# Decoder block with a 32-expert MoE in float32: consecutive weight rows per partition, and another order of work in the expert loop

## What is computed

```
logits = tok @ w_router + b_router;  vals, idx = top_k(logits, 4);  gates = softmax(vals)
for each of 32 experts:
    hgu   = tok @ w_gate_up[e] + b_gate_up[e]        # 1024 -> 2048, gate and up interleaved
    x_glu = min(hgu[:, 0::2], 7);  x_lin = clip(hgu[:, 1::2], -7, 7)
    act   = x_glu * sigmoid(1.702 * x_glu) * (x_lin + 1)
    acc  += gate[:, e] * (act @ w_down[e] + b_down[e])  # 1024 -> 1024
out = rms_norm(h + acc, g_final)
```

## Time and profile before

| what | us |
|---|---|
| runs of the kernel | 1122.81, 1123.18, 1124.02; median 1123.18 |
| profiled execution, its span | 1120.4 |
| profiled execution, its own time | not shown apart; the runs lie 2.4 to 3.6 above the span, their median 2.8 |
| TensorE busy | 1034.1 (92%) |
| VectorE, ScalarE, GpSimd busy | 253.4, 124.5, 45.2 |
| bytes moved | 420.09 MB, mean 375 GB/s |

### The profile page before, as it was taken

The page is one execution under the profiler, slowest core; times in us unless marked ns, Lnnn a source line. Parts: engine busy times, 40 slices in busy tenths (PEclk is TensorE's granted clock), DMA queues, the critical chain, the costliest instruction groups (busy, mean ns, idle before and its releaser), DMA issues.

```text
span 1120.4 us, 13552 instructions
## 1 busy us (share of the span) xinstructions
PE 1034.1 (92%) x5259; PEld 483.3 (43%) x5259; DVE 253.4 (23%) x648; ACT 124.5 (11%) x236; POOL 45.2 (4%) x85
## 2 busy tenths in 40 slices
PE   4979989999999999999999999999999999999995
PEld 3868454443444444433334444444444444444432
DVE  4886532111111111111111111111111111111102
ACT  2304321000000000000000000000000000000002
POOL 4830000000000000000000000000000000000000
PEclk9989979999999999999999999999999999999998
DMA  9972269999999999999999999999999999999891
GB/s 246 327 317 80 116 266 405 407 400 418 419 418 417 418 418 418 417 417 417 418 417 418 419 418 418 419 363 417 417 419 419 418 419 418 418 418 418 354 397 39
DMA packets 91783, 420.09 MB, mean 375 GB/s; under 512 B 7194, under 2 KB 23610, under 8 KB 58994
## 3 DMA queue, kind: packets, MB, share of 16 engines
q1 hardware_dynamic: 90646, 418.52, 93.0%
q0 software_dynamic: 1040, 1.20, 0.4%
q10 hardware_dynamic: 76, 0.09, 0.0%
HBM read 418.73 MB, written 1.05 MB: 375 GB/s over the span
## 4 chain that ended last, share of the span: by engine, by line
PE 88%; DVE 5%; ACT 4%; issue 1%; DMA 1%; SPq 0%; DVEq 0%
PE bank L1023 39%; PE bank L1053 20%; PE bank L996 11%; PE bank L1063 6%; DVE reg L621 4%; PE bank L882 3%; PE bank L928 2%; ACT reg L516 2%; ACT reg L518 2%; PE bank L1017 2%; PE bank L1041 1%; PE bank L1034 1%; DMA gu_ring<-in_conv_ln_b 1%; PE bank L864 0%; PE bank L1087 0%
## 5 line engine op out<-in xcount | busy, mean ns | idle before, releaser
L1023 PE MATMUL bank<-gu_ring,reg 128*64 128x512 f32 x2048 | 447.3, 594 | 0.0
L1023 PEld LDWEIGHTS bank<-gu_ring,reg 128*64 128x64 f32 x2048 | 145.9, 138 | 282.8 <-issue 277.3
L1053 PE MATMUL bank<-dn_ring,reg 128*64 128x512 f32 x1024 | 226.8, 595 | 26.8 <-ACT reg L516 26.8
L791 DVE TENSOR_SCALAR reg<-bank 128x256 f32<-128x256 f32 x64 | 24.2, 420 | 726.0 <-PE bank L1023 726.0
L1053 PEld LDWEIGHTS bank<-dn_ring,reg 128*64 128x64 f32 x1024 | 73.2, 137 | 159.8 <-issue 157.0
L996 PE MATMUL bank<-reg 128*128 128x64 f32 x1056 | 124.9, 278 | 0.9 <-DVE reg L690 0.9
L996 PEld LDWEIGHTS bank<-reg 128*128 128x128 f32 x1056 | 123.8, 196 | 1.0 <-issue 1.0
L1063 PE MATMUL bank<-reg 64*128 64x512 f32 x256 | 63.6, 615 | 22.1 <-ACT reg L518 22.1
L512 ACT ACTIVATE reg<-bank 128x256 f32<-128x256 f32 x32 | 12.3, 383 | 556.7 <-PE bank L1034 556.7
L882 PE MATMUL bank<-reg,gu_ring 128*128 128x272 f32 (+1 forms) x256 | 61.3, 402 | 0.6 <-issue 0.6
L882 PEld LDWEIGHTS bank<-reg,gu_ring 128*128 128x128 f32 x256 | 50.4, 197 | 11.1 <-DVE reg L584 1.0
(11 more groups left out here) (201 smaller groups left out, 381.2 us busy)
## 6 DMA issues: line engine op xcount, KB each, us to landing
gu_ring<-in_w_gate_up SPq DMA_DIRECT2D x256, 1024.0 KB, 17.1
dn_ring<-in_w_down SPq DMA_DIRECT2D x128, 1024.0 KB, 13.3
gu_ring<-in_w_in SPq DMA_DIRECT2D x16, 512.0 KB, 8.3
dn_ring<-in_w_out SPq DMA_DIRECT2D x4, 1024.0 KB, 11.2
xh<-in_x SPq DMA_DIRECT2D x2, 512.0 KB, 4.5
out<-gu_ring SPq DMA_DIRECT2D x4, 256.0 KB, 2.0
stage<-in_b_gate_up POOLq DMA_DIRECT2D x24, 32.0 KB, 5.3
gu_ring<-in_g_final SPq DMA_DIRECT2D x1, 512.0 KB, 5.6
```

The source lines that it names most:

```text
L791: ins = V.tensor_scalar(xglu[:, h], glu_v[:, :, 0], 7.0, None, ALU.min)
L1023: ins = mm(gub[b][64 * h:64 * h + 64, :], xgT[:, j, :], gu_ring[:, s, j, 1024 * h + 512 * b:1024 * h + 512 * b + 512], start=False, stop=( ...
L1053: ins = mm(db[64 * h:64 * h + 64, :], actT[:, at:at + SLOTS], dn_ring[:, k, 512 * h:512 * h + 512], start=(k == 0), stop=(k == KD - 1))
```

## The change

**Weight layout.** Gate/up rows are now `(p k) n`: partition p holds the 8 consecutive rows 8p to 8p+7, and a piece is two of them, 16 KB in a row from HBM. So there are 4 pieces of 2 MB (`GP = 4`, `PK = 2`) in place of 8 of 1 MB, and one release of a slot per two slices. From one partition to the next the address moves by 64 KB (before: 8 KB). Down rows are `(h p k) n`: a piece stays 1 MB, but a partition takes 8 KB in a row, at 16 KB from partition to partition. To fit this the normalised tokens `xn` are written with permuted features, the second norm's gain is loaded in the same order (`gffn`), and VectorE's reads of gate/up take a stride of 8 with half the columns each (`half`).

**Gather.** The one-hot is now stationary (64 columns) and the tokens stream, 512 columns at a time: 4 matmuls. The result has slots on the partitions, so ScalarE copies it (`gather_copy`) and TensorE transposes it with 4 more (`turn_gathered`).

**Combine.** That of expert n-1 now stands behind gate/up of expert n and the gather. The transposes of one-hot and activation go to the two gate/up banks.

**Biases.** `add_b_down` moves from behind expert 30 to behind expert 23, and its data is loaded by GpSimd at the start.

**End.** The length of the list is read ahead of the last combine; squares, gain and scaling are split over ScalarE and VectorE by token tile, and begin on the first tile while the second is combined. SyncE loads the final gain behind the last weights, not ahead of expert 31's gate/up.

```diff
-        actv = reg3[:, 512:1024]
+        xgn = reg3[:, 512:1024]
         xglu = reg3[:, 1024:1536]
         sigm = reg3[:, 1536:2048]
...
+        actv = lin
...
-        gu_v = w_gu[0].rearrange("e (k p) n -> p e k n", p=P)
-        dn_v = w_dn[0].rearrange("e (k p) n -> p e k n", p=P)
+        gu_v = w_gu[0].rearrange("e (p k) n -> e p (k n)", p=P)
+        dn_v = w_dn[0].rearrange("e (h p k) n -> e h p (k n)", h=2, p=P)
+        def gu_slot(s, j):
+            return gu_ring[:, s, PK * j:PK * (j + 1), :].rearrange("p k n -> p (k n)")
+        def gu_rows(e, j):
+            return gu_v[e, :, PK * F2 * j:PK * F2 * (j + 1)]
+        def dn_slot(j):
+            return dn_ring[:, 2 * j:2 * j + 2, :].rearrange("p k n -> p (k n)")
+        def dn_rows(e, j):
+            return dn_v[e, j // 2, :, 2 * D * (j % 2):2 * D * (j % 2 + 1)]
...
-                for j in range(KD):
-                    sp.wait_ge(gu_used[s], done * KD + (j + 1))
-                    sp.dma_start(gu_ring[:, s, j, :], gu_v[:, e, j, :]).then_inc(gu_in[s][j], 16)
+                for j in range(GP):
+                    sp.wait_ge(gu_used[s], done * GP + (j + 1))
+                    sp.dma_start(gu_slot(s, j), gu_rows(e, j)).then_inc(gu_in[s][j], 16)
...
-                    sp.dma_start(dn_ring[:, 2 * j:2 * j + 2, :], dn_v[:, e, 2 * j:2 * j + 2, :]).then_inc(dn_in[j], 16)
+                    sp.dma_start(dn_slot(j), dn_rows(e, j)).then_inc(dn_in[j], 16)
...
-            sp.wait_ge(gu_used[1], NE // 2 * KD)
-            sp.dma_start(bdn, b_dn[0]).then_inc(tail_in, 16)
-            sp.dma_start(gfin, g_final.partition_broadcast(P)).then_inc(gfin_in, 16)
             gu_load(0, NE - 1, NE // 2 - 2)
             dn_load(NE - 1, NE - 2)
+            sp.wait_ge(gu_used[1], NE // 2 * GP)
+            sp.dma_start(gfin, g_final.partition_broadcast(P)).then_inc(gfin_in, 16)
...
+            pool.dma_start(bdn, b_dn[0]).then_inc(tail_in, 16)
+            pool.dma_start(gffn[:, :], g_ffn[0].rearrange("(p k) -> p k", p=P)).then_inc(route_in, 16)
...
-                nc.scalar.activation(xn[:, t, :], xh[:, t, :], ACT.Copy, scale=rstd2[:, t:t + 1]).then_inc(xn_ok, 1)
+                nc.scalar.activation(xn[:, t, :].rearrange("q (h c p) -> q c h p", h=2, c=4),
+                                     xh[:, t, :].rearrange("q (p c h) -> q c h p", c=4, h=2), ACT.Copy, scale=rstd2[:, t:t + 1]).then_inc(xn_ok, 1)
...
-            def expert(n, first=False):
-                act.wait_ge(gT_ps, n + 1)
-                if not first:
-                    act.wait_ge(acc_ps, n)
-                nc.scalar.activation(gT, tb[:, 0:SEQ], ACT.Copy).then_inc(gT_ok, 1)
+            def gather_copy(n):
+                act.wait_ge(gath_ps, n + 1)
+                nc.scalar.activation(xgn, tb[:, :], ACT.Copy).then_inc(xgc_ok, 1)
+            gather_copy(0)
+            def expert(n):
                 act.wait_ge(glu_ok, n + 1)
                 nc.scalar.activation(sigm, xglu, ACT.Sigmoid, scale=1.702).then_inc(sg_ok, 1)
+                gather_copy(n + 1)
+                act.wait_ge(gT_ps, n + 1)
+                nc.scalar.activation(gT, gub[1][:, 0:SEQ], ACT.Copy).then_inc(gT_ok, 1)
                 act.wait_ge(aT_ps, n + 1)
-                nc.scalar.activation(actT, tb[:, :], ACT.Copy).then_inc(aT_ok, 1)
+                nc.scalar.activation(actT, gub[0][:, :], ACT.Copy).then_inc(aT_ok, 1)
...
             act.wait_ge(bd_ps, 1)
+            square(0, 0)
+            act.wait_ge(fin_ev, 1)
+            square(0, 1)
+            act.wait_ge(bd_ps, 2)
+            square(1, 0)
+            root(0)
+            act.wait_ge(fin_ev, 3)
+            square(1, 1)
+            scaled(0, 0)
+            root(1)
+            scaled(1, 1)
...
-                v.wait_ge(gath_ps, n + 1)
-                V.tensor_tensor(xgT[:, :, :], db[:, :].rearrange("p (k s) -> p k s", k=KD),
-                                colv[:, CC * NV + KD:].unsqueeze(2).to_broadcast([P, KD, SLOTS]), ALU.mult).then_inc(xg_ok, 1)
+                v.wait_ge(xT_ps, n + 1)
+                V.tensor_tensor(xgT[:, :, :], tb[:, :].rearrange("p (k s) -> p k s", k=KD),
+                                gffn[:, :].unsqueeze(2).to_broadcast([P, KD, SLOTS]), ALU.mult).then_inc(xg_ok, 1)
...
+                def half(a, b):
+                    return a.rearrange("p (k q) -> p k q", k=4)[:, :, 64 * b:64 * b + 64]
                 for b in range(2):
-                    glu_v = gub[b][:, :].rearrange("p (n two) -> p n two", two=2)
-                    h = slice(256 * b, 256 * b + 256)
-                    ins = V.tensor_scalar(xglu[:, h], glu_v[:, :, 0], 7.0, None, ALU.min)
+                    glu_v = gub[b][:, :].rearrange("p (q k two) -> p two k q", k=4, two=2)
+                    ins = V.tensor_scalar(half(xglu, b), glu_v[:, 0], 7.0, None, ALU.min)
                 ins.then_inc(glu_ok, 1)
                 for b in range(2):
-                    glu_v = gub[b][:, :].rearrange("p (n two) -> p n two", two=2)
-                    h = slice(256 * b, 256 * b + 256)
-                    ins = V.tensor_scalar(lin[:, h], glu_v[:, :, 1], 7.0, -7.0, ALU.min, ALU.max)
+                    glu_v = gub[b][:, :].rearrange("p (q k two) -> p two k q", k=4, two=2)
+                    ins = V.tensor_scalar(half(lin, b), glu_v[:, 1], 7.0, -7.0, ALU.min, ALU.max)
...
             def gather(n, after):
                 pe.wait_ge(oh_ok, after)
-                for k in range(KD):
-                    for t in range(TT):
-                        ins = mm(db[:, k * SLOTS:(k + 1) * SLOTS], xn[:, t, k * P:(k + 1) * P], onehot[:, t, :],
+                for t in range(TT):
+                    for h in range(2):
+                        ins = mm(tb[64 * h:64 * h + 64, :], onehot[:, t, :], xn[:, t, 512 * h:512 * h + 512],
                                  start=(t == 0), stop=(t == TT - 1))
                 ins.then_inc(gath_ps, 1)
+            def turn_gathered(n):
+                pe.wait_ge(xgc_ok, n + 1)
+                for c in range(4):
+                    ins = nc.tensor.transpose(tb[:, c * P:(c + 1) * P], xgn[:, c * P:(c + 1) * P], ident)
+                ins.then_inc(xT_ps, 1)
...
+            def combine(n, start=False, last=False):
+                pe.wait_ge(y_ok, n + 1)
+                for t in range(TT):
+                    for h in range(2):
+                        ins = mm(accb[t][h][:, :], gT[64 * h:64 * h + 64, t * P:(t + 1) * P], yv[64 * h:64 * h + 64, :],
+                                 start=start, stop=True, skip_group_check=True)
+                    if last:
+                        ins.then_inc(bd_ps, 1)
+            def expert(n, s, loads, before, start=False, between=None, before_turn=None, before_down=None):
 
                 pe.wait_ge(xg_ok, n * 2 + 2)
-                if not first:
-                    pe.wait_ge(gu_read, n)
+                if before is not None:
+                    pe.wait_ge(gT_ok, n)
+                    pe.wait_ge(aT_ok, n)
                 for b in range(2):
                     for h in range(2):
                         mm(gub[b][64 * h:64 * h + 64, :], selb[0:CAND, :], biasp[:, 1024 * h + 512 * b:1024 * h + 512 * b + 512],
                            start=True, stop=False)
                 for j in range(KD):
-                    pe.wait_ge(gu_in[s][j], loads * 16)
+                    if j % PK == 0:
+                        pe.wait_ge(gu_in[s][j // PK], loads * 16)
                     for b in range(2):
                         for h in range(2):
                             ins = mm(gub[b][64 * h:64 * h + 64, :], xgT[:, j, :],
                                      gu_ring[:, s, j, 1024 * h + 512 * b:1024 * h + 512 * b + 512],
                                      start=False, stop=(j == KD - 1))
-                    ins.then_inc(gu_used[s], 1)
+                    if j % PK == PK - 1:
+                        ins.then_inc(gu_used[s], 1)
                     if j == KD // 2 and between:
                         between()
                 if before_turn:
                     before_turn()
 
-                pe.wait_ge(oh_ok, n * 2 + 3)
+                gather(n + 1, n * 2 + 3)
+                if before is not None:
+                    combine(before, start)
+                pe.wait_ge(gu_read, n + 1)
                 for t in range(TT):
-                    ins = nc.tensor.transpose(tb[:, t * P:(t + 1) * P], wonehot[:, t, :], ident)
+                    ins = nc.tensor.transpose(gub[1][:, t * P:(t + 1) * P], wonehot[:, t, :], ident)
                 ins.then_inc(gT_ps, 1)
-                gather(n + 1, n * 2 + 3)
 
                 pe.wait_ge(act_ok, n + 1)
-                pe.wait_ge(gT_ok, n + 1)
                 for c in range(4):
-                    ins = nc.tensor.transpose(tb[:, c * P:(c + 1) * P], actv[:, c * P:(c + 1) * P], ident)
+                    ins = nc.tensor.transpose(gub[0][:, c * P:(c + 1) * P], actv[:, c * P:(c + 1) * P], ident)
                 ins.then_inc(aT_ps, 1)
```

(27 more changed lines are left out.)

140 lines of the change are left out of this document (88 added, 52 removed).

## The result

| what | before | after |
|---|---|---|
| median of the runs, us | 1123.39 (1122.81 to 1124.02, 4 runs) | 1081.29 (1080.10 to 1084.05, 4 runs) |
| ratio, 95% interval | | 0.9637 [0.9625, 0.9649] |
| profiled execution: own time, span | not shown apart, 1120.4 | 1080.82, 1079.0 |
| bytes moved, mean rate | 420.09 MB, 375 GB/s | 420.07 MB, 389 GB/s |

The account below looks back on a forecast made before the run. It took TensorE (29.24 us per expert) and the loads (30.04) as nearly equal bounds, with loads binding after: last gate/up landing at 1053, plus 15.8 to 1069, plus 9.8 is span 1079, plus 2.8 gives 1082 us; range 1068 to 1113.

Parts of the forecast that it names:

- Bounds: Per expert in the kernel before, TensorE needs 29.24 us and the loads 30.04, two bounds almost on top of each other.
- TensorE's chain: TensorE's work per expert, summed part by part: 29.24 us before, 26.6 after, at most 27.2 with the transposes.
- The loads: Weight stream after the change: 429 GB/s for 16 KB packets, 423 for 8 KB, 29.5 us per expert.
- the gain by packet size: About 9 ns per packet saved by larger packets; rival of no gain: period 30.04 us, 1098 us, chance 0.17.
- the pitch: Rival: reads 64 KB apart from partition to partition lower the loads' rate; at 399 GB/s 1142 us; chance 0.12.
- the 27 us: Extra time for the weight loads if the skill rule's 3% loss at large row pitches held at 64 KB.
- The clock rival: TensorE's clock falls through idle gaps where loads bind, costing about 8 us in the last expert: 1090; chance 0.08.
- About 3 us in each expert from the eighth on: Sign of being right: TensorE idle that long per expert on gate/up and down loads, experts 29.5 us apart.
- Issue to landing "falling early and then steady": Sign of being right: time from a weight load's issue to its landing falls early, then stays steady; no size given.
- The biases: The 8.4 us of `add_b_down` move into TensorE's slack and cost nothing; without that slack they'd cost 8.4.
- The start: First issue of expert 2's gate/up load at 164.7 us, bounds 163 and 166.5, for 163.07 before.
- The tail: From the copy of the last down's result to the end: 9.8 us in place of 14.2.

Follow-up runs that it names:

- e6: The change with the gather's 4 matmuls issued four times: 1200.95 us, ratio 1.0701 to the kernel before.
- e5: The change with the gather's 4 matmuls issued twice: 1094.05 us, ratio 0.9745 to the kernel before.
- e9: The change with the gather issued twice and the biases and residual behind expert 11 in place of 23: 1091.00 us.
- e3: The change with gate/up in 8 pieces of one row (1 MB, 8 KB packets), still 64 KB from partition to partition: 1090.42 us.
- e7: The change with down in two pieces of 2 MB, so that its packets are 16 KB too: 1081.51 us.
- e1: The change without its weight layout, with loop, biases, end and 2 MB pieces kept: 1100.35 us.
- the fillers: 4 unread matmuls in TensorE's idle stretches behind expert 1, added to the change with all small edits together: 1077.64 us, against 1078.00 without them.

## Why the prediction was right, and where its steps were not

- **Bounds: right.** The two nearly equal bounds were read from the rate of each kind of piece and from the growth of issue to landing. The layout alone (0 us) and the loop without it (23) confirm it from both sides, and TensorE made slower than the loads (e6) sets the pace again.
- **TensorE's chain: right.** 26.46 us per expert for 26.6. Ahead of all the L1097 together there are 0.7 us of idle time, those of the last combine; the activation's new order (L846 to L857) stays under the cover of gather and combine.
- **The loads: right.** 427 GB/s for 16 KB packets (429 estimated), 29.5 us per expert, first felt in expert 8. The rivals that were tested fall: the gain by packet size is there (30.1, 29.8, 29.5 and 29.4 us per expert with 8/4, 8/8, 16/8 and 16/16 KB packets for gate/up and down), and the pitch costs nothing that shows (422 GB/s with it, 423 without). The Trainium skill's rule on large row pitches (DMA: Bandwidth & Descriptors, Latency and other measured facts) isn't contradicted: no run here has a pitch of 512 KB, where its figures begin; the 27 us that the estimate read out of them at 64 KB did not come.
- **The clock rival: fell** for the stretch where the loads bind. PEclk is 1.00 in the profile's windows there, with pieces of 0.5 to 1.3 us idle between TensorE's bursts. One of the four executions had a lower mean clock (0.985) and took 1084.05; where it lost it, no profile shows.
- **"About 3 us in each expert from the eighth on": wrong behind the turn.** The step took the stream's period as the experts' period to the end. But at the turn down of n moves ahead of gate/up of n+1, and what TensorE needs next comes earlier: for seven experts, 20 to 26, it runs at 26.46 and doesn't wait. The end was right all the same, because TensorE catches up at expert 27; here the forecast had luck. It was a near thing: 12.7 us of margin, which the doubled gather used up. The claim that slack in TensorE is free wherever the loads bind was the real error, and two later expectations (e5, e9) rested on it. It fails in two places: behind the turn, and in the first experts, where TensorE's releases decide when the loads can be issued.
- **Issue to landing "falling early and then steady": wrong way.** It rises from 11.8 to 30.6 us while the faster TensorE asks earlier and earlier, and is steady once it waits for the loads (29.8 at 492:508). Behind the turn it is another figure, 34.6 near the end.
- **The biases: half.** They cost nothing where they are, but late they cost 5.4, not 8.4; the waits for the last pieces cover the rest. And the slack that they moved into is the margin of 12.7, which is counted with them in it.
- **The start: 1.8 us off.** First issue at 162.88 for 164.7 (the terms written there add to 164.6). The clock was 0.77 and not 0.55 in 150:165, and it moves from profile to profile of one kernel: in the change's second profile it was 0.96 and 1.00 in 155:160 and 160:165, for 0.75 and 0.90 in the first, and the first issue came at 161.37. **The tail: 0.6 short**, 10.4 for 9.8; the first square began 2.5 us behind the copy as forecast (2.6), and what follows took 7.9 for 7.2. The small misses nearly cancel: that the time was met to 1 us is partly luck, and the bounds of 1068 to 1113 say better what was known. (The lower one is a slip: a period of 29.1 in place of 29.5 is 12 us less, 1070.)

## To carry to other kernels

Where two resources are within a few per cent of each other, take the value of an edit from the other one's bound: an edit to either alone may be worth nothing (the layout, 0 us), and the pair more than the sum (42 for 23 + 0). Read the rate of a queue by kinds of packets, and watch issue to landing: if it grows from one round to the next, the queue is late, however busy TensorE is. And ask where the order of loads changes: behind such a place the same loop has another bound, and its margin must be counted apart. Before two kernels a few us apart are compared, compare executions of equal mean clock: the 3 us between e5 and e9 were 0.9.

## What the runs showed of the hardware that was not expected

**One core's weight loads run at 426 to 429 GB/s for 900 us.** Packets of 8 KB in place of 4 are worth 3% (411 to 423 GB/s in the kernel before), and packets of 16 KB in place of 8 for all weights another 1.7% (422 in e3, 429 in e7).

**The mean granted clock splits the executions of one kernel.** In the kernels with the new loop it is either 0.991 to 0.993 or 0.985 to 0.990, and the latter take longer. (The kernel before is at 0.986 to 0.988 in every execution.) Medians of the one and of the other, in us: the change 1080.6 (12 executions) and 1083.6 (2); without the layout 1099.3 (2) and 1101.5 (2); one-row pieces 1085.5 (1) and 1090.9 (3); gather twice 1091.9 (2) and 1095.8 (2); down in two pieces 1078.9 (1) and 1082.3 (4). Part of it is one place. Two profiles show the same stretch with and without a fall. One-row pieces, then the change (windows, columns as in the earlier trace rows):

```profile
215.00:220.00 5.00, 3.62 (x22) 2.22 (x20) 1.23 (x6) 0.60 (x1) 0.00 (x0) 0.80 1.01 421
220.00:225.00 5.00, 5.00 (x14) 1.58 (x12) 0.00 (x0) 0.00 (x0) 0.00 (x0) 0.52 0.90 351
```

```profile
215.00:220.00 5.00, 4.31 (x28) 2.45 (x29) 1.24 (x6) 0.00 (x0) 0.00 (x0) 1.00 1.01 424
220.00:225.00 5.00, 5.00 (x26) 1.87 (x23) 0.00 (x0) 0.00 (x0) 0.00 (x0) 1.00 1.05 429
```

In the one the clock goes to 0.50, that is from 2.4 to 1.2 GHz, from 218 to 224.5, behind the small matmuls that make the list of further items (2 stretches of 0.7 us idle about them). TensorE loses some 3 us, its releases come late, and the stream of loads falls to 351 GB/s and never gets that back: 2 us over 200:250. The rate of one-row pieces was measured beyond this place; its time in the one execution at the higher clock, 1085.5, is what was expected (1086). But this place is not all. The two profiles with the lower mean also have a lower clock at the start of the experts: in 155:160 it is 0.50 in both (one-row pieces, e1) for 0.75 in the change, and in e1 the first issue comes at 164.50 for 162.88. And a mean of 0.992 doesn't say that the clock held behind expert 1: in the profile of the doubled gather, at that mean, it is 0.50 from 220 to 222. That the idle stretches are the cause was tried with the fillers and is neither shown nor refuted: in their profile the clock held at 1.00 behind expert 1, two of five executions still had the lower mean, and where the clock fell in those two no profile shows. What brings it on stays open. So does how many of such executions a set of four holds, which is why medians here can be told apart to 2 or 3 us and no closer.
